# Running attention's value products and norm inside the input projection's last slab, and projecting attention first

## The chip, the cores and the metric

The kernel runs on one core of one Trainium2 chip (trn2). The metric is the device time of one execution, in microseconds. Three executions of the kernel before took 1712.12, 1700.7 and 1705.86 us, so the time before is 1705.86 us, the median. The profile and the trace come from one more execution, which took 1705.73 us.

## The reference

Two transformer blocks follow each other on a sequence of 256 tokens with 1024 features. Only the first block is touched. Cut to what matters:

```python
def first_block(x, c, ...):
    mod = jax.nn.silu(c) @ w_ada + b_ada          # six rows of 1024: shift, scale, gate, twice
    h = rms_norm(x, norm1_w) * (1.0 + scale1) + shift1
    q, k, v, cb, cc, cx, iq, ik, iw = jnp.split(h @ w_in, offs, axis=-1)
    q = rms_norm(q, q_norm_w); k = rms_norm(k, k_norm_w)
    y_attn = dsa_attention(q, k, v, iq, ik, iw)   # softmax over the chosen keys, then p @ v
    y_conv = short_conv(cb, cc, cx, conv_w, conv_b)   # cb * conv3(cc * cx)
    y_mix = jnp.concatenate([rms_norm(y_attn, attn_out_norm_w),
                             rms_norm(y_conv, conv_out_norm_w)], axis=-1)
    x = x + gate1 * (y_mix @ w_out)
    h2 = rms_norm(x, norm2_w) * (1.0 + scale2) + shift2
    return x + gate2 * peer_ffn(h2, ...)          # 8 heads x 16 experts a token out of 16384
```

`peer_ffn` multiplies `h2` by `peer_wq` (queries), takes scores against `subkeys`, chooses 16 experts a head and fetches the two rows of 1024 words of each chosen expert. The second block has modulation rows of its own (`w_ada_2`, 18 slabs), which depend only on its inputs `c` and so can be computed at any time before they are used.

## The kernel before

**Work and memory.** Activations lie feature-major, 128 features on the partitions and 256 tokens (two tiles of 128) along the free axis. Weights come in slabs of 128 x 4096 float32 words (2 MB), each a DMA on the SP queue, into a ring of four slots. SP issues the loads in one fixed order. Before most of them it waits until TensorE has read what the slot held; a load that waits holds up all loads behind it. Besides the ring, eight modulation slabs (numbers 12 and 14 to 20) are loaded into four spare homes in `arena` (`spare_slab`, home numbers in `SPARE_HOME`), by `load_spare(m)` in the same SP queue: 12 early, 14 after row 12 has been read (same home 3), 15 after the last piece of `w_in` has been read, 16 and 17 after `y_conv` and the last value product `pv3`, 19 after row 14 (home 3), 18 after row 15 (home 1), 20 after row 16 (home 2). In the code:

```python
if slabs[n][:2] == ("peer_wq", 2):
    sp.wait_ge(sem("y_conv"), 1)
    sp.wait_ge(group_done, index["pv3"] + 1)
    load_spare(16)
    load_spare(17)
    sp.wait_ge(*spare_read[14])
    load_spare(19)
    sp.wait_ge(*spare_read[15])
    load_spare(18)
    sp.wait_ge(*spare_read[16])
    load_spare(20)
```

**Rows.** `spare_row(m)` and `mod_steps` multiply one modulation slab by the condition (16 matmuls of 32 columns by 512 in the trace, since each float32 matmul shows as two passes there). `mod_turn` turns the finished rows of a group of up to four slabs back onto the partitions. Rows are filler work for TensorE: they stand wherever TensorE would wait.

**The stage of the change.** Engines run their own instruction streams, written out by hand and tied by semaphores; no scheduler moves anything. TensorE's stream ends the input projection with `cc`, `cx` and `cb` (two features-groups each; `cb` is the last slab of `w_in`). These are split products: ScalarE rounds each quarter slab (a piece) to a high part (line 1455), GpSimd subtracts it to get the low part (line 1374), and TensorE does three matmuls a block. Around them stand the attention steps: `turn_probs(t)` transposes the softmax of token tile t, `pv0` to `pv3` multiply it by the values (two heads each), `squares("conv")` and `squares("att")` sum squares for the two norms. `project` then multiplies `y_mix` by the two `w_out` slabs, tile 0 first (`wo0_0`, `wo0_1`). `second_norm(0)` sums squares of the new `x`, `query(0, 0)` makes the first queries, `turn_h(0)` transposes, `key_scores(0, 0)` makes the first scores. Then `project` does tile 1 (`wo1_0`, `wo1_1`), each releasing a `w_out` slot, into which SP loads `peer_wq` 2 and `w_ada_2` slab 9.

**The gathers.** VectorE takes the first scores and writes the first 16 expert numbers a token (`ids`, line 2413). GpSimd then issues one indirect DMA for each expert slot (line 1402): 128 rows of 8 KB, 1 MB. Eight row buffers overlay the spare homes, so the first four gathers wait until rows 17 and 18 have been copied out (`act.sem_inc`, line 1760), the next four until rows 19 and 20 have. There are 256 gathers; context slabs of the second block are loaded and multiplied in between. After the last gather the rest of the second block follows.

## Time and profile before

| | before |
|---|---|
| three executions, us | 1712.12, 1700.7, 1705.86 |
| profiled execution, us | 1705.73 |
| its span, first to last instruction, us | 1703.8 |
| TensorE busy | 1627.5 us, 96% |
| VectorE busy | 1167.1 us, 68% |
| ScalarE busy | 660.5 us, 39% |
| GpSimd busy | 389.6 us, 23% |
| chain that ended last | PE 62%, DMA 19%, DVE 10%, issue 6% |
| read from memory | 535.60 MB |

The span is 1.9 us shorter than the execution's own time; that part lies outside the instructions. PE is TensorE's matmuls and PEld its weight loads, DVE is VectorE, ACT ScalarE, POOL GpSimd, SPq the queue that issues most loads. PEclk is the granted TensorE clock as a share of full speed. "L518" is line 518 of the kernel, which is the helper `mm`, so nearly all matmuls carry it and are told apart by their tiles.

### The profile page before, as it was taken

What the parts mean: (1) busy time and instruction counts of PE and PEld (TensorE: products, weight loads), DVE (VectorE), ACT (ScalarE), POOL (GpSimd) and SP (SyncE); (2) the same over time, 40 slices, a digit from 0 to 9 for tenths busy, and PEclk for the clock granted to TensorE, in tenths of its full rate; (3) what the DMA queues carried; (4) which work ended last, traced back from release to release, by engine and by line L of the source; (5) the groups of instructions that cost most, each with busy time, mean ns of one, the idle gap of its engine ahead of it and who ended that gap; (6) DMA issues with size and microseconds to landing.
All of it is one profiled execution on the core that took longest, in us unless ns stands there. A gap on an engine that the chain in (4) does not pass through costs nothing.

```text
span 1703.8 us, 29036 instructions
## 1 busy us (share of the span) xinstructions
PE 1627.5 (96%) x11656; PEld 1464.0 (86%) x11656; DVE 1167.1 (68%) x1989; ACT 660.5 (39%) x1272; POOL 389.6 (23%) x317
## 2 busy tenths in 40 slices
PE   5999999988899899999998999999999999999997
PEld 3877889988899799998988567889998977989997
DVE  3675458778997677889788688564575456665554
ACT  3534133324433543433112158444434423444443
POOL 0553034434444434445343310000000000000000
PEclk9999999999999999999999999999999999999999
DMA  9868899999999999999999999865444522644442
GB/s 369 323 264 369 357 413 408 412 419 399 413 410 392 419 393 414 415 420 420 420 411 414 421 414 404 317 239 212 165 172 187 198 99 99 228 183 183 183 170 93
DMA packets 57732, 538.50 MB, mean 316 GB/s; under 512 B 6401, under 2 KB 6529, under 8 KB 7425
## 3 DMA queue, kind: packets, MB, share of 16 engines
q1 hardware_dynamic: 20592, 267.18, 39.5%
q0 software_dynamic: 37008, 269.50, 38.6%
q8 instruction: 92, 1.51, 0.4%
q14 instruction: 40, 0.32, 0.0%
HBM read 535.60 MB, written 1.05 MB: 315 GB/s over the span
## 4 chain that ended last, share of the span: by engine, by line
PE 62%; DMA 19%; DVE 10%; issue 6%; ACT 1%; POOL 1%; POOLq 0%; DVEq 0%; SPq 0%; ACTq 0%
PE psum L518 62%; DMA arena<-in_experts,idx_stage 16%; DVE arena L2538 4%; DVE arena L2527 1%; DMA ring<-in_w_ada 1%; POOL arena L1402 1%; DMA ring<-in_w_in 1%; DMA arena<-in_w_ada 1%; DMA extra_float<-in_w_ada 1%; DVE ring_r L2016 0%; POOL idx_stage L1395 0%; DVE arena L2649 0%; DVE small L2527 0%; DVE arena_r L2082 0%; ACT h_t L1832 0%
## 5 line engine op out<-in xcount | busy, mean ns | idle before, releaser
L2527 DVE CUSTOM_DVE_ANT_0 arena<-arena 128x1024 f32<-128x1024 f32 x256 | 313.8, 1226 | 133.5 <-DMA arena<-in_experts,idx_stage 127.4
L1402 POOL DMA_INDIRECT arena<-in_experts,idx_stage x256 | 303.8, 1187 | 365.7 <-DVE arena L2538 164.9
L2016 DVE TENSOR_TENSOR ring_r<-ring,ring_r 128x1024 fp32r<-128x1024 f32 (+1 forms) x200 | 240.7, 1214 | 197.0 <-ACT ring_r L1455 196.0
L518 PE MATMUL psum<-small_r,ring_r 128*128 128x256 f32 x1600 | 285.9, 283 | 3.4 <-DVE h_t_r L2097 3.4
L1455 ACT ACTIVATE ring_r<-ring 128x1024 fp32r<-128x1024 f32 (+1 forms) x200 | 208.2, 1048 | 170.4 <-PE psum L518 150.2
L518 PE MATMUL psum<-small,arena 128*128 128x128 f32 x2112 | 251.4, 280 | 22.0 <-ACT small L1858 21.7
L518 PEld LDWEIGHTS psum<-small,arena 128*128 128x128 f32 x2112 | 246.1, 196 | 25.9 <-ACT small L1858 23.0
L518 PEld LDWEIGHTS psum<-small_r,ring_r 128*128 128x128 f32 x1600 | 245.3, 189 | 5.4 <-issue 5.2
L518 PE MATMUL psum<-h_t,ring 128*128 128x256 f32 (+1 forms) x1360 | 248.1, 341 | 1.2 <-DMA ring<-in_w_in 1.2
L518 PEld LDWEIGHTS psum<-h_t,ring 128*128 128x128 f32 x1360 | 219.3, 191 | 21.9 <-DMA ring<-in_w_in 1.4
L518 PE MATMUL psum<-h_t_r,ring_r 128*128 128x256 f32 x800 | 223.8, 280 | 0.0
L518 PE MATMUL psum<-arena_r,ring_r 128*128 128x256 f32 x1488 | 211.6, 284 | 2.8 <-DVE arena_r L2082 2.8
L1920 ACT ACTIVATE small<-small 128x2 f32<-128x2 f32 x127 | 25.8, 203 | 463.9 <-DVE small L2527 463.8
L518 PEld LDWEIGHTS psum<-arena_r,ring_r 128*128 128x128 f32 x1488 | 192.9, 191 | 3.2 <-DVE arena_r L2082 3.2
L2538 DVE SCALAR_TENSOR_TENSOR arena<-arena,small 128x1024 f32<-128x1024 f32 x123 | 158.1, 1285 | 5.7 <-ACT small L1851 1.3
L518 PEld LDWEIGHTS psum<-h_t_r,ring_r 128*128 128x128 f32 x800 | 151.1, 189 | 0.1
L518 PE MATMUL psum<-arena,ring 128*128 128x128 f32 (+1 forms) x916 | 141.8, 316 | 0.0
L518 PEld LDWEIGHTS psum<-arena,ring 128*128 128x128 f32 x916 | 130.4, 192 | 10.7 <-issue 1.7
L518 PEld LDWEIGHTS psum<-ring 128*128 128x128 f32 x1056 | 122.9, 195 | 3.4 <-DVE ring L2478 1.9
L518 PE MATMUL psum<-ring 128*128 128x128 f32 x1056 | 123.2, 279 | 1.9 <-DVE ring L2478 1.7
L518 PE MATMUL psum<-ring_r,small_r 128*128 128x512 f32 x272 | 90.1, 399 | 0.8 <-DVE ring_r L2016 0.8
L518 PE MATMUL psum<-arena_r,upper 128*128 128x256 f32 x384 | 73.9, 295 | 9.9 <-DVE ring_r L2016 5.6
(281 smaller groups left out, 1687.6 us busy)
## 6 DMA issues: line engine op xcount, KB each, us to landing
ring<-in_w_in SPq DMA_DIRECT2D x31, 2048.0 KB, 8.6
ring<-in_w_ffn SPq DMA_DIRECT2D x29, 2048.0 KB, 11.2
ring<-in_w_ada SPq DMA_DIRECT2D x18, 2048.0 KB, 9.5
ring<-in_w_ffn SPq DMA_DIRECT2D x23, 1408.0 KB, 7.4
arena<-in_w_ada SPq DMA_DIRECT2D x8, 2048.0 KB, 16.4
ring<-in_w_out SPq DMA_DIRECT2D x4, 2048.0 KB, 9.3
ring<-in_peer_wq SPq DMA_DIRECT2D x4, 2048.0 KB, 10.3
extra_float<-in_w_ffn SPq DMA_DIRECT2D x4, 2048.0 KB, 12.5
```

The lines of the kernel that those rows point to most:

```text
L518: return nc.tensor.matmul(o, a, b, start=first, stop=last)
L1402: nc.gpsimd.indirect_dma_start(rows[slot % GBUF], None, dram["experts"], bass.IndirectOffsetOnAxis(ap=idx_stage[:, slot:slot + 1], axis=0) ...
L1455: nc.scalar.activation(upper(i), whole(i, ring), ACT.Copy).then_inc(hi_made, 1)
L1920: nc.scalar.activation(acts[:, n % 8, :], dots[:, n % 8, :], ACT.Gelu_apprx_tanh).then_inc(sem("gelus"), 1)
L2016: nc.vector.tensor_tensor(whole(i, ring_r), whole(i, ring), upper(i).bitcast(F32), ALU.subtract).then_inc(lo_made, 1)
L2527: step(nc.vector.tensor_tensor_reduce(u, u, h2[:, n // PER_TILE, :], 1.0, 0.0, ALU.mult, ALU.add, dots[:, n % 8, s:s + 1]), sem("dots"))
L2538: ins = STT(y_sum, row, weight, y_sum, ALU.mult, ALU.add)
```

## The change

TensorE now transposes both tiles' probabilities at once, right after `cx`. Then comes the first half of `cb`, then all four value products, then the second half of `cb`, then attention's squares, row 12, the convolution's squares and row 13. The output projection takes attention's blocks first. Row 14 stands behind `wo0_1`, row 15 behind `second_norm(0)`, rows 16 to 18 together behind `key_scores(0, 0)` and ahead of `wo1_0`. ScalarE's stream follows this order: it takes the two exponentials (`exp_probs`) earlier, copies the values' products out ahead of the convolution's squares, and loads the square root's table by an instruction of its own (`root_table`). Attention's squares get a place of their own (`sq_att`, where `gate_c` lay), and the convolution's root one of its own (`rstd_conv`, in `h_words`). SP's and GpSimd's instructions, and the matmuls themselves, are the same in number and in their own order.

```diff
+        sq_att = arena[:, 4096:5120].rearrange("p (j t) -> p j t", j=KA)
+        rstd_conv = h_words[:, 0:L]
...
             turn_probs(0)
-            split_feature("cb", 2, h1_hi, h_lo_1, "dve")
-            spare_row(12)
             turn_probs(1)
-            mod_steps(13, 14, False)
+            split_feature("cb", 1, h1_hi, h_lo_1, "dve")
             pe.wait_ge(*emptied("pt1_3"))
             for j in range(KA):
...
                 end(last)
-                if j == 1:
-                    squares("conv", sq1, KA, "act")
-            spare_row(14)
-            squares("att", sq1[:, KA:KD, :], KA, "act")
+            split_feature("cb", 1, h1_hi, h_lo_1, "dve", start=1)
+            squares("att", sq_att, KA, "act")
+            spare_row(12)
+            squares("conv", sq1, KA, "act")
+            mod_steps(13, 14, False)
...
                     if t == 0:
-                        pe.wait_ge(sem("y_mix"), (k - KA if k >= KA else k + KA) + 1)
+                        pe.wait_ge(sem("y_mix"), k + 1)
                     for j in range(4):
                         last = mm(o[:, j * P:(j + 1) * P], w_out[i][0][:, k, j * P:(j + 1) * P], y_mix[:, t, k, :],
-                                  k == KA and j == 0, k == KA - 1 and j == 3)
+                                  k == j == 0, k == KD - 1 and j == 3)
...
             for i in range(2):
-                project(out_banks[i], 0, i, range(KA, KD))
+                project(out_banks[i], 0, i, range(KA))
             for i in range(2):
-                end(project(out_banks[i], 0, i, range(KA)))
+                end(project(out_banks[i], 0, i, range(KA, KD)))
+            spare_row(14)
+            second_norm(0)
             spare_row(15)
-            second_norm(0)
-            spare_row(16)
...
             key_scores(0, 0)
+            spare_row(16)
+            spare_row(17)
+            spare_row(18)
             for i in range(2):
-                end(project(begin(f"wo1_{i}", "dve"), 1, i, [*range(KA, KD), *range(KA)]))
+                end(project(begin(f"wo1_{i}", "dve"), 1, i, range(KD)))
                 release(n=w_out[i][1])
-                if i == 0:
-                    spare_row(17)
-                    spare_row(18)
             spare_row(19)
...
-            for i in range(2):
-                copy_out(f"cc{i}", flat(gate_c[:, 2 * i:2 * i + 2, :]))
-            mod_steps(9, 10, False)
-            for t in range(NT):
-                exp_probs(t)
-                ahead(f"cx{t}")
+            copy_out("cc0", flat(gate_c[:, 0:2, :]))
+            ahead("cc1")
+            exp_probs(0)
+            copy_out("cc1", flat(gate_c[:, 2:4, :]))
+            mod_steps(9, 10, False)
+            exp_probs(1)
+            for i in range(2):
+                ahead(f"cx{i}")
...
+            for j in range(KA):
+                copy_out(f"pv{j}", y_att[:, j, :], width=L)
+            act.wait_ge(drained["act"], taken[0])
+            act.wait_ge(*emptied("cx1"))
+            square("att", sq_att, y_att, KA)
+            root_table()
             act.wait_ge(sem("y_conv"), 1)
             square("conv", sq1, y_conv, KA)
+            norm_root("att", ATT)
+            mod_steps(12, 13, False)
+            norm_root("conv", ATT, dst=rstd_conv)
             mod_steps(13, 14, False)
-            for j in range(KA):
-                copy_out(f"pv{j}", y_att[:, j, :], width=L)
-                if j == 1:
-                    norm_root("conv", ATT)
...
-            rooted_norm("conv")
-            mix(y_conv, KA, param("conv_out_norm_w"))
-            rooted_norm("att")
-            mix(y_att, 0, param("attn_out_norm_w"))
+            rooted_norm("att", rstd[:])
+            mix(y_att, 0, param("attn_out_norm_w"), rstd[:])
+            rooted_norm("conv", rstd_conv)
+            mix(y_conv, KA, param("conv_out_norm_w"), rstd_conv)
```

The order of the matmuls on TensorE between the input projection's last slab and the output projection, before. `arena,silu 32x512` is a row from a spare home, `ring,silu` one from the ring, `early,small` a turn, `64x128` a value product, `arena,ones` a sum of squares, `arena,ring 128x128` the output projection:

```order
L518 MATMUL psum<-arena,silu 32x512 x8
L518 MATMUL psum<-early,small 128x2 x4
L871 MATMUL psum<-early,h_t 128x128 x16
L518 MATMUL psum<-ring,silu 32x512 x8
L518 MATMUL psum<-arena 64x128 x12
L518 MATMUL psum<-arena,ones 128x256 x4
L518 MATMUL psum<-arena 64x128 x12
L518 MATMUL psum<-arena,silu 32x512 x8
L518 MATMUL psum<-arena,ones 128x256 x4
L518 MATMUL psum<-arena,ring 128x128 x64
```

The same place in the changed kernel, from the end of the last slab (its last matmul is the first row) on:

```order
L520 MATMUL psum<-arena_r,ring_r 128x256
L520 MATMUL psum<-arena,ones 128x256 x4
L520 MATMUL psum<-arena,silu 32x512 x8
L520 MATMUL psum<-early,small 128x2 x4
L520 MATMUL psum<-arena,ones 128x256 x4
L520 MATMUL psum<-ring,silu 32x512 x8
L520 MATMUL psum<-arena,ring 128x128 x64
```

The transposes (16) and value products (24) have gone ahead, into the last slab, and row 14 has gone behind the projection; rows 12 and 13 have stayed. 

TensorE from the output projection of tile 0 to that of tile 1, before. `h_t,ring` is the first query, `L969` the transposes, `arena 128x128` the first scores:

```order
L518 MATMUL psum<-arena,ring 128x128 x64
L518 MATMUL psum<-arena,silu 32x512 x8
L518 MATMUL psum<-arena,ones 128x128 x8
L518 MATMUL psum<-arena,silu 32x512 x8
L518 MATMUL psum<-early,small 128x8 x4
L518 MATMUL psum<-h_t,ring 128x128 x32
L969 MATMUL psum<-early,h_t 128x128 x8
L518 MATMUL psum<-arena 128x128 x4
L518 MATMUL psum<-arena,ring 128x128 x32
L518 MATMUL psum<-arena,silu 32x512 x16
L518 MATMUL psum<-arena,ring 128x128 x32
```

And in the changed kernel:

```order
L520 MATMUL psum<-arena,ring 128x128 x64
L520 MATMUL psum<-arena,silu 32x512 x8
L520 MATMUL psum<-arena,ones 128x128 x8
L520 MATMUL psum<-arena,silu 32x512 x8
L520 MATMUL psum<-h_t,ring 128x128 x32
L970 MATMUL psum<-early,h_t 128x128 x8
L520 MATMUL psum<-arena 128x128 x4
L520 MATMUL psum<-arena,silu 32x512 x8
L520 MATMUL psum<-early,small 128x8 x4
L520 MATMUL psum<-arena,silu 32x512 x16
L520 MATMUL psum<-arena,ring 128x128 x64
```

The row that stands alone behind the first `arena,ring` is 15 before and 14 now; the one behind the squares is 16 before and 15 now. Row 16 and the turn of rows 12 to 15 have gone behind the first scores, and rows 17 and 18 stand ahead of `wo1_0` instead of between the two halves.

## Rows read from the trace of the kernel before

**Rows 1.** The profile page's first line.

```profile
span 1703.8 us, 29036 instructions
```

**Rows 2.** Busy time by window: window, PE, PEld, DVE, ACT, POOL, PEclk, DMA, GB/s.

```profile
211.00:1040.00 829.00, 793.33 (x5348) 716.17 (x5341) 665.44 (x1270) 289.98 (x753) 328.52 (x289) 0.99 1.00 412
1040.00:1704.00 664.00, 644.28 (x4846) 595.15 (x4844) 384.56 (x497) 289.88 (x385) 0.00 (x0) 0.99 0.50 190
```

**Rows 3.** Timeline of TensorE: start, duration, operation, count, idle time before.

```profile
142.50 1.09 PE L871 MATMUL psum<-early,arena 128*128 128x128 f32 x8
...
154.95 1.92 PE L518 MATMUL psum<-arena,silu 128*32 128x512 f32 x16
...
157.72 1.95 PE L871 MATMUL psum<-early,h_t 128*128 128x128 f32 x16
...
161.45 1.53 PE L518 MATMUL psum<-arena 128*64 128x128 f32 x24
162.91 1.99 PE L518 MATMUL psum<-arena,ones 128*128 128x256 f32 x8
...
167.46 1.92 PE L518 MATMUL psum<-arena,silu 128*32 128x512 f32 x16 [1.10 <-DMA arena<-in_w_ada]
...
171.15 14.46 PE L518 MATMUL psum<-arena,ring 128*128 128x128 f32 x128
185.53 1.92 PE L518 MATMUL psum<-arena,silu 128*32 128x512 f32 x16
...
189.37 1.92 PE L518 MATMUL psum<-arena,silu 128*32 128x512 f32 x16
...
192.13 7.39 PE L518 MATMUL psum<-h_t,ring 128*128 128x128 f32 x64
```

**Rows 4.** The same timeline, later.

```profile
201.22 7.31 PE L518 MATMUL psum<-arena,ring 128*128 128x128 f32 x64
...
219.38 1.92 PE L518 MATMUL psum<-arena,silu 128*32 128x512 f32 x16
```

**Rows 5.** Timeline of VectorE.

```profile
123.99 3.88 DVE L2283 TENSOR_TENSOR h_t<-h_t,small 128x2048 f32<-128x2048 f32 x1
...
140.73 2.29 DVE L2287 TENSOR_REDUCE small<-h_t 128x8 f32<-128x2048 f32 x1 [6.85 <-ACT h_t L1685]
...
156.16 1.41 DVE L2314 TENSOR_TENSOR arena<-arena,psum 128x512 f32<-128x512 f32 x2
...
167.30 2.05 DVE L2171 SCALAR_TENSOR_TENSOR arena<-arena,prm,rstd 128x256 f32<-128x256 f32 x4
```

**Rows 6.** Timeline of VectorE at the first expert list.

```profile
211.51 0.17 DVE L2413 CAST ids<-small 128x16 uint32<-128x16 f32 x1
```

**Rows 7.** Timeline of ScalarE at the second norm.

```profile
191.32 2.44 ACT L1734 ACTIVATE h_t<-h_t,mod 128x128 f32<-128x128 f32 x8 [1.48 <-DVE h_t L2345]
```

**Rows 8.** Busy time in windows of 4 us; columns as in rows 2.

```profile
152.00:156.00 4.00, 4.00 (x38) 3.23 (x40) 3.71 (x9) 0.00 (x0) 0.00 (x0) 1.00 0.55 233
...
188.00:192.00 4.00, 4.00 (x36) 2.44 (x36) 2.02 (x6) 1.41 (x5) 0.00 (x0) 1.00 1.00 426
...
200.00:204.00 4.00, 4.00 (x37) 3.93 (x36) 1.95 (x14) 1.73 (x4) 0.00 (x0) 1.00 0.83 348
204.00:208.00 4.00, 4.00 (x38) 4.00 (x37) 3.69 (x15) 0.00 (x0) 0.00 (x0) 1.00 0.02 8
208.00:212.00 4.00, 4.00 (x37) 1.29 (x36) 3.59 (x13) 0.00 (x0) 0.00 (x0) 1.00 0.61 176
```

**Rows 9.** Timeline of the SP queue: when loads were issued.

```profile
155.05 0.33 SPq L1350 DMA_DIRECT2D ring<-in_peer_wq  x1
...
166.47 25.21 SPq L1313 DMA_DIRECT2D arena<-in_w_ada  x5
```

**Rows 10.** DMA issues of 180 to 190 us: KB, us to landing.

```profile
arena<-in_w_ada SPq DMA_DIRECT2D x1, 2048.0 KB, 12.9
```

**Rows 11.** Timeline of GpSimd at the first gather.

```profile
213.57 1.12 POOL L1402 DMA_INDIRECT arena<-in_experts,idx_stage  x1 [0.98 <-POOL idx_stage L1395]
```

More of the change, by code:

```diff
@@ L1436, in root, with norm_root @@
                 nc.scalar.activation(ap, ap, ACT.Sqrt).then_inc(sem("root_out"), 1)
-            def norm_root(tag, n=D, tokens=slice(0, L)):
-                drain(nc.scalar.activation(rstd[:, tokens], take("ss_" + tag)[:, tokens], ACT.Sqrt, bias=eps, scale=1.0 / n))
+            def norm_root(tag, n=D, tokens=slice(0, L), dst=None):
+                drain(nc.scalar.activation((rstd if dst is None else dst)[:, tokens], take("ss_" + tag)[:, tokens], ACT.Sqrt, bias=eps, scale=1.0 / n))
             hi_count = [0]
@@ L1737, in _ @@
             square_tile(0)
-            mod_steps(15, 16, False)
+            mod_steps(14, 15, False)
             second_root(0)
             second_normed(0)
-            mod_steps(16, 17, False)
+            mod_steps(15, 16, False)
             def copy_query(t, i):
@@ L1758, in _ @@
             copy_scores(0, 0)
-            mod_steps(17, 19, False)
+            mod_steps(16, 19, False)
             act.sem_inc(sem("row_free_pe"), GBUF // 2)
@@ L2167, in tile_ff_dve, with mix @@
                               ALU.mult, ALU.add))
-            def mix(src, k0, weight):
+            def mix(src, k0, weight, root):
                 for j in range(KA):
                     step(STT(y_mix[:, :, k0 + j, :], src[:, j, :].rearrange("p (t n) -> p t n", t=NT), weight[:, j:j + 1],
-                             rstd[:].rearrange("p (t n) -> p t n", t=NT), ALU.mult, ALU.mult), sem("y_mix"))
+                             root.rearrange("p (t n) -> p t n", t=NT), ALU.mult, ALU.mult), sem("y_mix"))
             def residual(names, dst, gate, per, after, sq=sq2):
@@ L2290, in normalise, with rooted_norm @@
                      sem("probs"))
-            def rooted_norm(tag):
+            def rooted_norm(tag, root):
                 v.wait_ge(*emptied("ss_" + tag))
-                step(nc.vector.reciprocal(rstd[:], rstd[:]))
+                step(nc.vector.reciprocal(root, root))
             logits(0)
```

6 lines of the change are left out of this document (removed).

## The prediction

> **What bounds the kernel now.** I read the page's first line [rows 1], then windows, then timelines of the stage that changes. From 211 to 1040 us, while the 256 expert gathers and the context slabs run, the DMA engines are busy 1.00 of the time at 412 GB/s [rows 2]. TensorE is busy 793 of 829 us there too, so two resources run side by side, but the DMA engines never pause. Behind 1040 us they are half idle (0.50) and TensorE is busy 644 of 664 us [rows 2]: a tail bound by TensorE, whose instructions the change leaves alone. Before 211 us the reader should look for holes in the DMA traffic, because a saturated phase ends when its bytes are through: a change moves the end of the kernel by as much as it changes the holes ahead of that phase. The holes stand in the 4 us windows [rows 8]: 152 to 156 is busy 0.55, 200 to 204 0.83, 204 to 208 0.02, 208 to 212 0.61. At 426 GB/s, the rate of a full window in the same rows, the three windows from 200 to 212 moved (348 + 8 + 176) x 4 us, 2.13 MB, which is 5.0 us of work, so 7.0 us are idle; the one from 152 has 1.8 us.
>
> **What a load costs.** A slab is 2.097 MB, so 4.93 us at 426 GB/s. Loads of the SP queue land in the order of issue: slab 18 was issued when row 15 had been read, at 185.53 + 1.85 = 187.4 us [rows 3], and landed 12.9 us later [rows 10], at 200.4. From 155.05, the issue of the first `peer_wq` slab [rows 9], to then the queue carried that slab, 14, the subkeys (half a slab), 15, `peer_wq` 1, 16, 17, 19 and 18, together 8.5 loads or 41.9 us, and 155.05 + 41.9 = 197.0; what is left, 3.4 us, is start and landing. So this queue had no hole, and all of it moves by as much as its first load.
>
> The Trainium skill (DMA: Bandwidth & Descriptors, Anatomy of one DMA) gives about 2.0 us fixed and then 436 GB/s for a DMA. By that the 8.5 loads take 40.9 us and slab 18 would land 1.0 us sooner than the rows say; the measured landing decides. The same skill (SBUF — State Buffer, A bandwidth-pool intuition that's wrong) says that device memory is almost always the bottleneck, at some 358 GB/s a core, which speaks against a gain from any reordering of engines; the trace agrees with the first and not with the figure, since rows 2 show 412 over 829 us.
>
> **TensorE through the stage.** Steps are timed from one row's start to the next's. The first transposes and both halves of `cb` take 154.95 - 142.50 = 12.45 us, a row 1.85 (the last to the next row's start), a turn 0.92, the 16 transposes of tile 1 1.87, each half of the value products 1.46, a sum of squares 1.9, a projected tile 14.4 [rows 3]. Changed kernel, from 142.50 on:
> - Transposes, `cb`, value products: 12.45 + 1.87 + 2.92 = 17.24, so `cb` ends at 159.75, not 154.95. This needs the probabilities of tile 1 by 143.4. Now VectorE starts their sum at 140.73, after waiting 6.85 us for ScalarE's exponential [rows 5], which stands behind a wait for a weight slab. In the new order that exponential comes ahead of the slab, and VectorE's shifted logits are ready at 123.99 + 3.88 = 127.9 [rows 5]; the exponential can end near 130. VectorE's steps for tile 1 are a sum (2.29), a small reciprocal and a product, which I bound by the 3.88 of the subtraction of the same shape; those of tile 0 have half the elements. Together 6.4 + 3.4, so done by 137.7 to 139. No wait, with 4 us of margin.
> - `y_conv` needs the second half of `cb`: VectorE's two products take 1.41 [rows 5], so the last one ends at about 160.5. The square and the root follow while TensorE does attention's squares (to 161.6), row 12 (163.45), its turn (164.4), the convolution's squares (166.2) and row 13 (168.05). Attention's root comes at 162.1, its reciprocal takes 1.75 and its four products 2.05 [rows 5], so they are done at 166.0, before the projection asks. The convolution's follow 4.5 us later and are asked for 7.2 us later. No wait; and the wait of 1.10 for slab 14 [rows 3] is gone, since row 14 is now asked for at 182.45.
> - Projection 168.05 to 182.45 (171.15 to 185.53 before: 3.1 us ahead). Row 14 takes row 15's old place, the squares end at 186.3 instead of 189.37, row 15 at 188.15.
> - The first query before had 2.76 us of cover, from 189.37 to 192.13 (row 16 and a turn). The chain from the squares to the first normed block ends at 191.32 + 0.38 = 191.7 [rows 7], 2.33 us after the squares. Now only row 15 covers it, 1.85: a new wait of 0.5. The query starts at 188.65, the first scores end at 188.65 + 9.1 = 197.75, against 201.22: 3.45 us ahead.
> - Rows 16 to 18 and a turn: 16 to 199.6, the turn to 200.5, 17 to 202.4. Row 18 then waits (below).
>
> **The loads, which are the other side.** All SP loads behind `cb` are held longer, since SP waits for the last piece of `w_in`, for row 12 and for row 13, all later now. The first goes out at 159.9 instead of 155.05: a longer hole by **+4.85 us**. Slab 14 goes out after row 12 (163.5), `peer_wq` 1 after row 13 (168.2), 16 and 17 right behind, 19 after row 14 (184.4), 18 after row 15 (188.2); each is there before the traffic ahead of it ends (17 ends about 193), so no further hole opens. Slab 18 lands at 200.4 + 4.85 = 205.2. TensorE, which wants it at 202.4, waits **2.8 us**. Row 18 ends at 207.1, `wo1_1` at 221.5, against 219.38 [rows 4]: TensorE, 3.45 us ahead at the scores, enters the gather phase 2.1 us behind. `peer_wq` 2 goes out when `wo1_0` is read, at 214.3 instead of 208.5.
>
> Slab 20 goes out after row 16, at 199.7, and its traffic ends at 203.3 + 4.85 = 208.2, the old end of traffic [rows 8] moved.
>
> The first gathers need the first expert list and the copies of rows 17 and 18. The list comes 10.5 us after the scores (211.68 - 201.2) [rows 4, 6], at 208.2 instead of 211.7; row 18 is copied at 207.8. So the list decides, and with a copy and 0.98 us behind it the first gather, issued at 213.57 before [rows 11], goes out at about 209.5; its traffic starts near 210.6. The hole there is 208.2 to 210.6, **2.4 us instead of 7.0**. Behind it four gathers (9.9 us) and `peer_wq` 2 fill the engines to 225, `w_ada_2` slab 9 (221.6) to 230, and the next four gathers go out near 227.
>
> **Sum.** Holes: +4.85 - 4.6 = **+0.3 us**. The same bytes follow. On the profiled execution, 1705.73 us with 1.9 us outside the span, that is 1706.0; on the median of 1705.86 it is 1706.2. I forecast **1706 us**, no change. The gain on TensorE and the earlier gathers are paid for by loads that start later.
>
> **Unknown costs.** How much of TensorE's 2.1 us of delay gets through lies between 0 (TensorE pauses 36 us in the 829, so it has slack) and 2.1; I take 0, nearest to the row that shows DMA at 1.00. The conflict of VectorE and GpSimd while the convolution's chain runs beside the splits may stretch that chain, but it has from 138 to 159.8 for a chain that began behind tile 1's product (143 at the earliest, 140.73 + 2.29) and ended at 156.16 [rows 5]. It would have to take 21 us instead of at most 13, so 0. Below zero: if gathers wait for their own round trip more than for bandwidth, their start 4.1 us sooner (213.57 to 209.5) counts in full, otherwise not at all; rows 2 are nearest to not at all.
>
> **Rivals.**
> - *Slower: row 18 late, and TensorE's delay counts.* The place is `spare_row(18)`; the price is 0.3 + 2.1 = 2.4 us, 1708.3, and up to 5 where slab 18 lands 3 us later still. It decides if the DMA backlog around 238 us runs out: by my sum the second four gathers end at 240.2 and the next slab's traffic starts at 239.7, a margin of half a microsecond. For it: that margin, and that TensorE is busy 96% of the phase. Against it: TensorE's 36 us of pauses.
> - *Faster: gathers bound by their own latency.* If each gather's round trip and not bandwidth sets the pace, the phase starts 4.1 us sooner: 1705.9 - 4.1 = 1701.8. For it: 19% of the chain that ended last is DMA. Against it: DMA busy 1.00 at 412 GB/s for 829 us.
> - *The transposes of tile 1 wait.* If the exponential isn't freed by the new order, TensorE stands at 143.4 until the old 146.2, 2.8 us, and `cb` and all loads behind move with it: 1706.2 + 2.8 = 1709. For it: ScalarE still stands behind one piece before it. Against it: 4 us of margin.
>
> **How the numbers follow.** A measurement of this kernel can tell about 1% (17 us) from no change, and the three executions lie within 11.4 us. Chances: forecast (within 1.5 us of 1706) 0.55, slower rival 0.22, faster rival 0.13, waiting transposes 0.06, something else 0.04. The cases reach from 1701.8 to 1709 and 1711 with the slower one's upper price; the scatter of a median of such executions adds a few microseconds at the low end. Range 1700 to 1711. No case comes to 17 us, so: faster by over 1% 0.02, within 1% 0.95, slower by over 1% 0.03.
>
> **What would show it.** The first `peer_wq` slab issued near 160 and a window before it nearly empty; no wait for `probs`; the first scores about 197.8; TensorE idle 2 to 3 us for a DMA into `arena` ahead of row 18; the first gather issued near 209.5; `wo1_1` ending near 221.5; DMA at 1.00 from 211 to 1040 and the last gather at the same time as before. I am wrong if the last gather lands more than 3 us from where it did with the DMA share still 1.00, or if TensorE's idle time in the phase grows.

## The result, and the profile of the changed kernel

The changed kernel took 1709.26 us in the median of 13 executions (1705.87 to 1716.49), the kernel before 1704.91 us in 13 executions beside it (1700.7 to 1712.12). The ratio is 1.0026, with a 95% interval of 1.0015 to 1.0038: it is 4.4 us slower, by 2.6 to 6.5. A second comparison, told below, gave 1.0049 (1.0033 to 1.0065). Both are within the 1% called "no change", and both are on the slow side of zero. The profiled execution took 1708.66 us, with a span of 1706.9 us.

TensorE's timeline in the changed kernel, the counterpart of [rows 3] and [rows 4] (start, duration, operation, count, and in brackets the idle time before it and what ended it):

```profile
159.94 1.89 PE L520 MATMUL psum<-arena,ones 128*128 128x256 f32 x8
161.76 1.92 PE L520 MATMUL psum<-arena,silu 128*32 128x512 f32 x16
...
168.28 14.56 PE L520 MATMUL psum<-arena,ring 128*128 128x128 f32 x128
...
189.10 7.38 PE L520 MATMUL psum<-h_t,ring 128*128 128x128 f32 x64 [0.57 <-ACT h_t L1736]
...
198.28 1.92 PE L520 MATMUL psum<-arena,silu 128*32 128x512 f32 x16
...
205.90 3.24 PE L520 MATMUL psum<-arena,silu 128*32 128x512 f32 x16 [2.85 <-DMA arena<-in_w_ada]
209.06 14.56 PE L520 MATMUL psum<-arena,ring 128*128 128x128 f32 x128
223.55 1.93 PE L520 MATMUL psum<-arena,silu 128*32 128x512 f32 x16
...
230.95 7.39 PE L520 MATMUL psum<-h_t,ring 128*128 128x128 f32 x64
239.07 1.92 PE L520 MATMUL psum<-ring,silu 128*32 128x512 f32 x16 [0.73 <-ACT arena L1479]
...
241.92 3.74 PE L520 MATMUL psum<-small,arena 128*128 128x128 f32 x32
```

The same place in the kernel before:

```profile
234.10 1.92 PE L518 MATMUL psum<-ring,silu 128*32 128x512 f32 x16
...
237.24 3.84 PE L518 MATMUL psum<-small,arena 128*128 128x128 f32 x32
```

The reader should see three delays in a row. TensorE stands 2.85 us for slab 18. Then row 18 takes 3.24 us, where every other row takes 1.92. And row 21, which is the `ring,silu` row at 239.07, waits 0.73 us for a copy of ScalarE. The first expert products begin at 241.92 instead of 237.24, 4.68 us later. This is where the long phase starts for TensorE.

The load queue (SP) and GpSimd's gathers, as [rows 9] and [rows 11]; the second fence is GpSimd:

```profile
160.13 0.33 SPq L1351 DMA_DIRECT2D ring<-in_peer_wq  x1
...
216.50 0.33 SPq L1351 DMA_DIRECT2D ring<-in_peer_wq  x1
223.65 0.33 SPq L1351 DMA_DIRECT2D ring<-in_w_ada  x1
```

```profile
210.61 1.12 POOL L1403 DMA_INDIRECT arena<-in_experts,idx_stage  x1 [0.98 <-POOL idx_stage L1396]
...
229.56 0.94 POOL L1403 DMA_INDIRECT arena<-in_experts,idx_stage  x1 [14.10 <-ACTq L1903]
```

The first gather goes out 2.96 us sooner than in [rows 11]; the fifth, which needs the homes of rows 19 and 20, at 229.56 instead of 225.11, 4.45 us later. So the early start is lost again within four gathers.

Busy time by window in the changed kernel, columns as in [rows 2] and [rows 8]:

```profile
152.00:156.00 4.00, 4.00 (x57) 3.83 (x52) 1.59 (x3) 2.87 (x6) 0.00 (x0) 1.00 0.68 287
156.00:160.00 4.00, 4.00 (x36) 4.00 (x35) 0.00 (x0) 1.22 (x2) 0.00 (x0) 1.00 0.00 0
...
204.00:208.00 4.00, 2.10 (x12) 0.59 (x16) 3.62 (x13) 0.00 (x0) 0.00 (x0) 0.65 1.03 438
208.00:212.00 4.00, 4.00 (x34) 2.94 (x27) 3.73 (x24) 2.10 (x3) 1.30 (x2) 0.93 0.10 41
212.00:216.00 4.00, 4.00 (x39) 4.00 (x38) 0.54 (x2) 0.00 (x0) 2.82 (x3) 1.00 0.88 297
211.00:1040.00 829.00, 790.23 (x5359) 713.78 (x5358) 657.32 (x1247) 283.84 (x746) 327.36 (x288) 0.99 1.00 410
```

To count the holes I take the bytes of four windows in a row at 426 GB/s, as in the prediction, and call the rest of the 16 us idle. From 152 to 168 it is 2.4 us before and 7.0 now, from 200 to 216 it is 7.4 before and 4.8 now; together 9.8 before and 11.8 now, 2.0 us more. In the phase the DMA share is 1.00, as in [rows 2], but 410 GB/s instead of 412. Over 829 us that is about 1.7 MB less, 4 us of traffic. The share hides this; the rate shows it. The last gather went out at 994.18 instead of 988.33.

### The profile page after: what moved, and what is told of

Its sections match the earlier page's. It is cut to its first block, busy times and chain, and to the rows that moved or that the text cites. A ratio compares the mean times of both kernels' runs of the same rounds, so it can differ in the third digit from the quotient of the medians.

```text
span 1706.9 us, 29037 instructions
## 1 busy us (share of the span) xinstructions
PE 1625.9 (95%) x11656; PEld 1459.4 (86%) x11656; DVE 1170.2 (69%) x1989; ACT 661.4 (39%) x1273; POOL 387.4 (23%) x317
## 4 chain that ended last, share of the span: by engine, by line
PE 59%; DMA 20%; DVE 11%; issue 7%; ACT 2%; POOL 1%; POOLq 0%; DVEq 0%; SPq 0%; ACTq 0%
PE psum L520 59%; DMA arena<-in_experts,idx_stage 17%; DVE arena L2540 4%; DVE arena L2529 2%; DMA arena<-in_w_ada 1%; DMA ring<-in_w_ada 1%; POOL arena L1403 1%; DMA ring<-in_w_in 1%; DMA extra_float<-in_w_ada 1%; DVE ring_r L2018 0%; DVE small L2529 0%; DVE arena L2651 0%; DVE arena_r L2084 0%; ACT h_t L1834 0%; DVE arena L2357 0%
## 5 line engine op out<-in xcount | busy, mean ns | idle before, releaser
L1456 ACT ACTIVATE ring_r<-ring 128x1024 fp32r<-128x1024 f32 (+1 forms) x200 | 208.2, 1048 | 168.4 <-PE psum L520 148.4
```

The lines of the kernel that those rows point to most:

```text
L1456: nc.scalar.activation(upper(i), whole(i, ring), ACT.Copy).then_inc(hi_made, 1)
```

## The experiments

All ratios are to the kernel before, run beside each; "us" is the ratio's distance from 1 times 1705. A ratio is estimated over all executions and isn't the quotient of the two medians, from which it differs by up to 0.0009. The first four answer whether TensorE's delay or the holes in the load traffic cost the time.

**Rows 17 and 18 back between the halves of `wo1`, all else changed.**

```diff
             spare_row(16)
-            spare_row(17)
-            spare_row(18)
             for i in range(2):
                 end(project(begin(f"wo1_{i}", "dve"), 1, i, range(KD)))
                 release(n=w_out[i][1])
+                if i == 0:
+                    spare_row(17)
+                    spare_row(18)
```

> The changed kernel with one part undone: rows 17 and 18 stand between the two halves of the tile 1 projection again, as before; everything else is as changed. Theory 1 (TensorE enters the gather phase late, 241.9 instead of 237.2 us, because row 18 waits 2.85 us for its slab and then runs at a lower granted clock): the wait goes, TensorE is level with the kernel before at the end of the projection (about 219.5), and the time is that of the kernel before, ratio 1.000 within 0.001. Theory 2 (the DMA engines carry 5 us less before 211 us, since all loads behind the last input slab start 4.85 us later): this stays as it is, the first gathers even go out at 213.5 again, so the ratio to before stays at 1.002 to 1.003.

Measured: 1704.23 us, ratio 0.9996 (0.9984 to 1.0008). TensorE's timeline of this kernel:

```profile
201.00 7.39 PE L520 MATMUL psum<-arena,ring 128*128 128x128 f32 x64
208.32 3.64 PE L520 MATMUL psum<-arena,silu 128*32 128x512 f32 x32
...
219.23 1.92 PE L520 MATMUL psum<-arena,silu 128*32 128x512 f32 x16
```

The two rows have no wait and their 3.64 us are at full clock. SP issued `peer_wq` 0 at 160.08, as late as in the changed kernel, and the first gather went out at 213.43. So the late loads stay, the first gather is back at its old time, TensorE's delay is gone, and with it the loss. But the extra holes are gone as well. Counted as above, the idle time is 7.1 + 2.4 = 9.5 us, like the 9.8 of the kernel before: the later loads now run on until `peer_wq` 2 follows them, issued at 208.42, so the second hole shrinks by as much as the first has grown. The expectation took the holes to stay as in the changed kernel, and they don't, so this run shows that the place of rows 17 and 18 is the cause, and doesn't tell TensorE's delay from the holes.

**Slab 15 loaded ahead of `peer_wq` 0, all else changed.**

```diff
+                if slabs[n][:2] == ("peer_wq", 0):
+                    sp.wait_ge(group_done, index["pt0_1"] + 1)
+                    load_spare(15)
                 if slabs[n][:2] == ("peer_wq", 1):
...
-                    sp.wait_ge(group_done, index["pt0_1"] + 1)
-                    load_spare(15)
```

> The changed kernel with the load of slab 15 issued ahead of the first peer_wq load, as soon as the transposes of tile 0 are done (about 144 us), so that it runs in the hole of DMA traffic from 154 to 162 us. Every later load lands 4.9 us sooner, slab 18 at about 201. Theory 1 (late TensorE): the wait ahead of row 18 is gone, the projection of tile 1 ends near 219.2, TensorE is 0.5 us ahead of before: ratio to before 0.999 to 1.000. Theory 2 (bytes carried ahead of the gathers): the hole is filled while the first gathers stay 3 to 4 us ahead, so 2.5 us are gained on before: ratio 0.998 to 0.999.

Measured: 1705.04 us, ratio 1.0005 (0.9996 to 1.0015). Timeline of its load queue, then of TensorE:

```profile
143.26 0.33 SPq L1314 DMA_DIRECT2D arena<-in_w_ada  x1
159.40 0.33 SPq L1352 DMA_DIRECT2D ring<-in_peer_wq  x1
```

```profile
200.39 3.64 PE L520 MATMUL psum<-arena,silu 128*32 128x512 f32 x32
...
218.45 1.92 PE L520 MATMUL psum<-arena,silu 128*32 128x512 f32 x16
```

A slab sooner in the queue, and slab 18 is there when TensorE asks. TensorE is 0.9 us ahead of the kernel before, 218.45 against 219.38 [rows 4]; 0.7 of that is this execution's, whose row 12 starts at 161.03 instead of 161.76. The first gather goes out at 209.15, near the 209.5 that I had forecast for the changed kernel. The loss is gone, but no gain takes its place. The second theory's gain of 2.5 us isn't there, and neither is what it rests on, since the hole isn't filled but moved: from 196 to 200 us the rate is now 205 GB/s instead of 418, and from 152 to 168 and 196 to 216 together 10.7 us are idle, against 9.9 in the kernel before.

**Rows 17 and 18 ahead of `wo1_0` in the kernel before.**

```diff
             key_scores(0, 0)
+            spare_row(17)
+            spare_row(18)
             for i in range(2):
...
-                if i == 0:
-                    spare_row(17)
-                    spare_row(18)
```

> The kernel before with one small part of the change: rows 17 and 18 stand ahead of both halves of the tile 1 projection. Slab 18 has landed at 200.4, so TensorE does not wait and ends the projection at 219.4 as before, but the w_out slot is read 3.6 us later, so the third peer_wq load goes out at 212.2 instead of 208.6 and the DMA traffic has a hole 3.6 us longer. Theory 1 (late TensorE): no change, ratio 1.000. Theory 2 (holes in the DMA traffic): 3.6 us slower, ratio 1.002.

Measured: 1707.09 us, ratio 1.0012 (1.0001 to 1.0024), 2.0 us. Busy time by window:

```profile
204.00:208.00 4.00, 4.00 (x39) 2.27 (x32) 3.83 (x20) 1.54 (x2) 0.00 (x0) 1.00 0.19 78
208.00:212.00 4.00, 4.00 (x38) 4.00 (x37) 3.62 (x13) 0.34 (x1) 0.00 (x0) 1.00 0.00 0
212.00:216.00 4.00, 4.00 (x38) 4.00 (x38) 3.76 (x23) 0.21 (x1) 1.62 (x3) 1.00 0.42 98
```

TensorE waits nowhere more than before, but `peer_wq` 2 is issued at 213.69 instead of 208.56, 3.6 us of it since `wo1_0` is read later and 1.5 us since this execution's row 12 starts at 156.45 instead of 154.95. The idle time from 200 to 216 is 10.3 us instead of 7.4, and with 2.5 us of the first stretch 12.8 instead of 9.8. The measured 2.0 us fit these 3.0 us of holes, but the interval reaches almost to zero. So holes aren't free; this one is likely paid for.

**20 matmuls more (4.5 us) in the second query of the kernel before.**

```diff
+                if (t, i) == (0, 1):
+                    for n, (j, k) in enumerate(order[:20]):
+                        mm(o[:, j * P:(j + 1) * P], w[:, k, j * P:(j + 1) * P], h_t[:, k, t * P:(t + 1) * P], n == 0, n == 19)
```

> The kernel before with 20 matmuls more ahead of the second query of tile 0 (the first 20 of that query made twice, the result is the same), some 4.5 us of TensorE work, behind all rows and loads of the changed stage. The first gathers, the loads up to then and the holes ahead of them stay as before; TensorE enters the gather phase 4.5 us later. Theory 1 (late TensorE): 4 to 4.5 us slower, ratio 1.0025. Theory 2 (holes): 0 to 1 us, ratio 1.000.

Measured: 1710.27 us, ratio 1.0029 (1.0019 to 1.0040), 4.9 us. TensorE's timeline:

```profile
226.80 11.86 PE L518 MATMUL psum<-h_t,ring 128*128 128x128 f32 x104
238.59 1.92 PE L518 MATMUL psum<-ring,silu 128*32 128x512 f32 x16
```

No load and none of the first eight gathers is later here (`peer_wq` 2 at 208.59, slab 9 at 219.51); TensorE alone is 4.5 us late, and the kernel takes 4.9 us longer. What comes behind is late too: the next `peer_wq` load goes out at 240.58 instead of 236.08, the ninth gather at 245.32 instead of 241.22. Busy time by window, in the kernel before and then in this one:

```profile
216.00:300.00 84.00, 83.87 (x745) 79.11 (x745) 61.62 (x164) 32.18 (x94) 31.96 (x32) 1.00 1.00 413
```

```profile
216.00:300.00 84.00, 83.87 (x745) 79.11 (x744) 57.56 (x155) 28.79 (x86) 30.42 (x31) 1.00 0.99 392
```

TensorE is as busy as before, and the DMA engines move 21 GB/s less for 84 us, 4.1 us of traffic. This is how a delay of TensorE alone becomes a delay of the loads, and it is the step that I had priced at nothing.

**20 of 32 matmuls left out of the second query, in the kernel before and in the changed one.** Only 3 of the 8 blocks of features are summed, so a part of the chosen experts differ. The same edit in both:

```diff
+                kd = 3 if (t, i) == (0, 1) else KD
-                order = [(j, k) for j in range(4) for k in range(KD)] if by_head else \
+                order = [(j, k) for j in range(4) for k in range(kd)] if by_head else \
...
```

> The kernel before, with 20 of the 32 matmuls of the second query of tile 0 left out (only the first 3 of 8 blocks of features are summed, so part of the chosen experts differ): TensorE enters the gather phase 4.5 us earlier, some 229.6 instead of 234.1 us. Theory 1 (the phase is paced by TensorE): 4 to 4.5 us faster, ratio 0.9975. Theory 2 (the phase is bound by the bytes of the DMA engines, which have little to spare): no gain or under 1 us, ratio 0.9995 to 1.000.

> The changed kernel with the same 20 matmuls left out (the same part of the second query is missing): TensorE reaches the gather phase at 234.6 instead of 239.1 us, level with the kernel before at 234.1, while the holes in the DMA traffic stay as in the changed kernel. Theory 1 (lateness of TensorE is the whole cost): ratio to before 1.000, within 0.001. Theory 2: ratio stays at 1.002 or more.

Measured: in the kernel before 1703.61 us, 0.9988 (0.9973 to 1.0002); in the changed kernel 1707.02 us, 1.0008 (0.9994 to 1.0023). The first interval holds both forecasts for it, 0.9975 and 0.9995 to 1.000, so the time doesn't decide; the trace says more. TensorE's timeline of the kernel before with the edit, then of the changed kernel with it:

```profile
227.51 2.92 PE L518 MATMUL psum<-h_t,ring 128*128 128x128 f32 x24
233.33 3.52 PE L518 MATMUL psum<-ring,silu 128*32 128x512 f32 x16 [2.90 <-DMA ring<-in_w_ada]
...
237.78 3.74 PE L518 MATMUL psum<-small,arena 128*128 128x128 f32 x32
```

```profile
224.03 1.93 PE L520 MATMUL psum<-arena,silu 128*32 128x512 f32 x16
...
237.22 3.21 PE L520 MATMUL psum<-ring,silu 128*32 128x512 f32 x16 [2.87 <-DMA ring<-in_w_ada]
```

Here the asymmetry has its reason. TensorE gets through 4.5 us sooner, then stands 2.90 us for slab 9, the slab of row 21, and takes 1.60 us longer for this row, slowly: the first products begin at 237.78, no sooner than before. The DMA issues of the kernel before from 219 to 221 us are slab 9 alone, issued at 219.48 (KB, us to landing):

```profile
ring<-in_w_ada SPq DMA_DIRECT2D x1, 2048.0 KB, 12.6
```

So the slab is there at 232.1, and TensorE reaches row 21 at 234.10, 2.0 us behind it. TensorE is the later of the two, so a delay of its own has no cover, and a lead of more than 2 us meets a wait. In the changed kernel SP can issue slab 9 only when `wo1_1` has been read, at 223.65 instead of 219.48: the delay travels by the loads as well. With the short query it is issued at 224.13, row 21 starts at 237.22 and the first products at 241.36, still 4.0 us late. The ratio of 1.0008 is what theory 1 asked for, but TensorE's delay wasn't taken away, so the run doesn't speak for it.

**40 matmuls more (9 us)**, the loop above with 40 in place of 20, the blocks beginning again after 32.

> The kernel before with 40 matmuls more at the same place instead of 20, 9 us of TensorE work. Theory 1 (TensorE paces the phase, no slack): 9 us slower, ratio 1.0053. If TensorE's pauses in the phase, 36 us of 829, absorbed part of a delay, the second 4.5 us would cost less than the first; under theory 2 the cost would begin only where the DMA backlog runs out.

Measured: 1715.27 us, ratio 1.0045 (1.0028 to 1.0061), 7.7 us (4.8 to 10.4). Twice the delay costs 1.6 times as much by the middle values; the intervals allow full and half.

**Slab 15 early and another PSUM bank for the second query.** The load's edit as above, and one bank skipped, so that row 21 doesn't come to a bank that is still being copied out:

```diff
             mod_turn(unturned.pop(0))
+            at_bank[0] += 1
             for _ in query(0, 1):
```

> The changed kernel with the load of slab 15 issued ahead of the first peer_wq load, as in the run with that label, and with the PSUM bank of the second query shifted by one, from bank 7 to bank 2. In the changed kernel the query lies in one of the two banks that are set aside for the sums of expert rows, and TensorE waits 0.73 us for its copy. Theory 1: the wait goes, TensorE is 0.7 to 1.2 us ahead of before, ratio to before 0.9993 to 1.000. Theory 2: no effect of the bank; ratio 0.998 to 0.999 by the filled hole alone, which the run without the bank shift did not show.

Measured: 1705.37 us, ratio 0.9990 (0.9977 to 1.0003). The wait of 0.73 us is gone:

```profile
234.78 1.92 PE L520 MATMUL psum<-ring,silu 128*32 128x512 f32 x16
```

It is the best version of the change that I ran, and it isn't told from the kernel before.

**TensorE's delay taken away or added ahead of the end of `wo1_1`, and the changed kernel once more.** The first edit, of the changed kernel, leaves out five of the eight blocks of `wo1_1`, 20 of its 32 matmuls; the second, of the kernel before, adds 20 whose sums are overwritten:

```diff
-                end(project(begin(f"wo1_{i}", "dve"), 1, i, range(KD)))
+                end(project(begin(f"wo1_{i}", "dve"), 1, i, [0, 1, KD - 1] if i else range(KD)))
```

```diff
             def project(o, t, i, blocks):
+                if (t, i) == (1, 1):
+                    for n in range(20):
+                        j, k = n % 4, n // 4
+                        mm(o[:, j * P:(j + 1) * P], w_out[i][0][:, k, j * P:(j + 1) * P], y_mix[:, t, k, :], n == 0, n == 19)
```

> The changed kernel, but the second half of the output projection of tile 1 (wo1_1) multiplies three of its eight blocks, so 20 of its 32 matmuls (4.5 us) are left out, and TensorE's delay is gone ahead of everything that waits for this product: the load of slab 9 into its slot, rows 19 and 20, and the gathers 4 to 7 that need these rows' homes. The loads ahead of it stay as late as in the changed kernel. Theory A, TensorE's delay is passed on by two ways, its own instructions and what it releases: both ways are closed, wo1_1 ends near 219.1, the fifth gather goes out near 225.1, slab 9 is issued near 219.2, the first expert products start near 238, and the ratio to the kernel before is 1.000 (0.999 to 1.001), below the 1.0008 of the kernel whose query was shortened behind these releases. Theory B, about a third of the loss is the holes of the loads: 1.001 or more.

> The kernel before with 20 matmuls more (4.5 us) ahead of wo1_1, whose sums are overwritten, so nothing of the result changes. TensorE is late ahead of the releases instead of behind them as in the run with 20 more in the second query. Theory A, the delay counts in full by either way: ratio 1.0027 (1.0015 to 1.004), the same as with the matmuls in the query, and the same as the changed kernel: wo1_1 ends near 223.9, fifth gather near 229.6, slab 9 issued near 224, first products near 241.7. Theory B, what hurts is the sum of late releases and a late TensorE, each in part by itself: the loads behind make it more than in the query, 1.004 or more.

> The changed kernel once more beside the other two, for the same chip and the same runs of the kernel before. All theories: 1.0026 within 1.0015 to 1.0038, which is what its first comparison gave. A ratio below 1.001 would mean that the first comparison overstated the loss and that the theories explain too much.

Measured, in this order: 1707.49 us, 1.0013 (1.0002 to 1.0024); 1710.50 us, 1.0034 (1.0021 to 1.0047); 1711.79 us, 1.0049 (1.0033 to 1.0065).

The middle one agrees with theory A: 4.5 us ahead of the releases cost 5.8 us (3.6 to 8.0), about as much as behind them; it has five executions, and its interval reaches theory B's 1.004 too. The first misses theory A's 1.000 by a little and lies where theory B had it. Its load queue and TensorE show that it doesn't decide between them:

```profile
218.60 0.33 SPq L1351 DMA_DIRECT2D ring<-in_peer_wq  x1
221.28 0.33 SPq L1351 DMA_DIRECT2D ring<-in_w_ada  x1
```

```profile
207.68 2.75 PE L520 MATMUL psum<-arena,silu 128*32 128x512 f32 x16 [2.99 <-DMA arena<-in_w_ada]
...
238.23 2.58 PE L520 MATMUL psum<-ring,silu 128*32 128x512 f32 x16 [2.27 <-DMA ring<-in_w_ada]
```

`peer_wq` 2 still goes out late, behind `wo1_0`, now 2.7 us ahead of slab 9, and slab 9 lands behind it: TensorE waits for it again. The edit took the delay out of TensorE's work but not out of the loads, and the first products are still 3.7 us late. The third is the changed kernel's second comparison, with six executions, and it misses the 1.0015 to 1.0038 that I expected. Its interval and the first comparison's overlap from 1.0033 to 1.0038. The loss is real in both, and its size is known to a factor of two. The profiled execution of this comparison was its fastest, 1703.96 us. TensorE's timeline there:

```profile
204.67 1.92 PE L520 MATMUL psum<-arena,silu 128*32 128x512 f32 x16 [2.60 <-DMA arena<-in_w_ada]
...
221.02 1.92 PE L520 MATMUL psum<-arena,silu 128*32 128x512 f32 x16
```

The wait for slab 18 is there (2.60 us), but row 18 takes 1.92 us, and the first products begin at 239.39.

**The wait for slab 18 filled with matmuls.**

```diff
             def spare_row(m):
+                if m == 18:
+                    bank = cycle[at_bank[0] % len(cycle)]
+                    if bank in tenant:
+                        pe.wait_ge(*tenant[bank])
+                    for n in range(12):
+                        mm(psum[:, bank, 0:P], ones[:], ones[:], n == 0, n == 11)
```

> The changed kernel, with 12 matmuls of ones by ones (128x128, some 2.7 us, results overwritten and never read) on TensorE ahead of its wait for slab 18. Nothing of the result changes, all loads and gathers keep their places, and row 18 starts when the slab lands, as in the changed kernel; only TensorE computes where it stood still. Theory A, only the time at which row 18 and what follows it run counts: row 18 starts near 205.9 again, and the ratio stays at what the changed kernel gave, 1.0026 or more (its two comparisons gave 1.0026 and 1.0049). Theory C, the lower granted clock behind the wait is a part of the loss (row 18 took 3.24 us at a granted clock of 0.50 in one profile of the changed kernel, 1.92 at 1.00 in another, and its executions had a mean granted clock of 0.985 against 0.986 to 0.987 of the kernel before): row 18 takes 1.92 us, wo1_1 ends 1.3 us sooner, near 222.2, the mean granted clock of the executions rises by 0.001, and the ratio falls to 1.001 to 1.002. If the filler itself is late and pushes row 18 back by more than half a microsecond, the run tells nothing between the two.

Measured: 1709.11 us, ratio 1.0019 (1.0004 to 1.0034), and a mean granted clock of 0.9861, against 0.9863 of the kernel before beside it and 0.9849 and 0.9847 in the two comparisons of the changed kernel. TensorE's timeline, then one window of this kernel and the same one of the changed kernel:

```profile
199.74 1.92 PE L526 MATMUL psum<-arena,silu 128*32 128x512 f32 x16
...
204.44 2.94 PE L526 MATMUL psum<-ones 128*128 128x128 f32 x24
207.31 1.92 PE L526 MATMUL psum<-arena,silu 128*32 128x512 f32 x16
209.16 14.56 PE L526 MATMUL psum<-arena,ring 128*128 128x128 f32 x128
```

```profile
206.00:208.00 2.00, 2.00 (x21) 1.48 (x23) 1.76 (x8) 0.00 (x0) 0.00 (x0) 1.00 0.96 410
```

```profile
206.00:208.00 2.00, 2.00 (x12) 0.48 (x16) 1.86 (x5) 0.00 (x0) 0.00 (x0) 0.50 1.08 459
```

From the start of row 16 to the start of `wo1_0` it takes 209.16 - 199.74 = 9.42 us instead of 209.06 - 198.28 = 10.78: 1.36 us sooner, with 2.9 us of work more. In the trace theory C is right: the lower clock behind the wait cost 1.3 us in the changed kernel's first profile. The measured time fits it (1.001 to 1.002 was asked for), but its interval holds theory A's 1.0026 too, so in the time it isn't told apart.

**All runs side by side.** Executions of one kernel differ by up to 2.6 us in where the stage stands already at row 12, so the delay of the first expert products is taken from row 12's start: products minus 237.24, less row 12's start minus 154.95 (161.76, as in the changed kernel's first profile, for versions of it). Of the changed kernel's 4.7 us 0.36 stand already ahead of the changed place, where its first transposes begin at 142.86 instead of 142.50, and the same is in the rows of its versions. The third column is the traffic that is missing at 300 us: the bytes from 140 us on, in windows of 4 us shifted by the same start of row 12, taken from those of the kernel before and divided by 426 GB/s.

| kernel | delay of first products, us | traffic missing at 300 us, us | measured, us (interval) |
|---|---|---|---|
| changed, first comparison | 4.7 | 4.2 | 4.4 (2.6 to 6.5) |
| changed, second comparison | 3.1 | 2.9 | 8.4 (5.6 to 11.1) |
| changed, wait filled | 3.3 | 2.9 | 3.2 (0.7 to 5.8) |
| changed, rows 17 and 18 between | 0.4 | 0.4 | -0.7 (-2.7 to 1.4) |
| changed, slab 15 early | 0.3 | 0.1 | 0.9 (-0.7 to 2.6) |
| changed, slab 15 early, other bank | -0.2 | 0.6 | -1.7 (-3.9 to 0.5) |
| changed, short `wo1_1` | 3.7 | 3.2 | 2.2 (0.3 to 4.1) |
| changed, short query | 4.0 | 3.4 | 1.4 (-1.0 to 3.9) |
| before, rows 17 and 18 ahead | -0.1 | 1.5 | 2.0 (0.2 to 4.1) |
| before, short query | -0.1 | 0.2 | -2.0 (-4.6 to 0.3) |
| before, +20 in the query | 4.4 | 4.1 | 4.9 (3.2 to 6.8) |
| before, +20 ahead of `wo1_1` | 4.7 | 4.6 | 5.8 (3.6 to 8.0) |
| before, +40 in the query | 9.1 | 8.7 | 7.7 (4.8 to 10.4) |

Ten of thirteen intervals hold the delay; two miss it by 0.1 and 0.3 us. Eleven hold the missing traffic, and one misses it by 0.1 us; it also covers the one kernel whose TensorE is on time and which still loses, rows 17 and 18 ahead. This column shows where holes and delay meet. With TensorE on time a hole ahead of the gathers is made up in part: 2.9 us are missing at 216 us and 1.5 at 300 with rows 17 and 18 ahead, 1.3 and 0.1 with slab 15 early. With TensorE late it grows: 2.4 and 4.2 us in the changed kernel, 0.0 and 4.1 with 20 matmuls more. The one far off by both is the second comparison, where one execution, the fastest of six, was profiled: a trace tells of its own execution, not of the median.

## Why the prediction came out as it did

The time of 1709.26 us lies in the range, and "within 1%" is right. That much was safe, since the range was drawn over the rivals and no case came near 17 us; the second comparison's median, 1711.79, is just outside the range. The forecast case, 1706 us with nothing moved, is not what happened: the slower rival is, at the place that it named.

- *Ahead of row 18 the steps held.* `cb` ended at 159.94 (forecast 159.75), the projection began at 168.28 (168.05), row 14's turn came at 182.77 (182.45), the new wait ahead of the query was 0.57 us (0.5), the scores ended at 198.28 (197.75). Nobody waited for `probs`.
- *The late loads held.* `peer_wq` 0 went out at 160.13 (159.9), and TensorE waited 2.85 us for slab 18 (2.8).
- *The first gather came at 210.61 (209.5)*, since row 18 was now later than the list of experts (`ids` at 208.47, forecast 208.2). The hole at 160 grew by 4.6 us (forecast 4.85), the one ahead of the gathers shrank by 2.6, where I had 4.6. So the holes sum to +2.0 us instead of +0.3.
- *The failed step* is "How much of TensorE's 2.1 us of delay gets through lies between 0 ... and 2.1; I take 0". The experiments show a delay getting through in full: 4.5 us added on TensorE alone cost 4.9 us (3.2 to 6.8), and 4.5 us ahead of the releases 5.8 (3.6 to 8.0). I took TensorE's 36 us of pauses in the phase for slack. They are elsewhere: in the kernel before TensorE is 88.87 of 89 us busy from 211 to 300, and the next thing that it needs, slab 9, has been there for 2.0 us when it comes, so nothing covers a delay. And the gathers and the next load wait for what TensorE's work sets free, so the delay becomes one of the traffic: with 20 matmuls more the ninth gather is 4.1 us late and 4.1 us of traffic are missing at 300 us.
- *The size was off as well*: `wo1_1` ended 4.17 us late (223.55 against 219.38), not 2.1. Of the difference 1.3 us is row 18 at a lower clock, and 0.7 us the slab's start at 205.90 instead of 205.2. Then 0.73 us is the wait for the PSUM bank, since the second query has slipped by one place into a bank that row 21 uses again; neither the lower clock nor the bank was in my sum. By the rival's own price, 0.3 + 2.1, it would have been 1708.3; the 4.7 us that the trace shows lie within the first comparison's 2.6 to 6.5. The holes' 2.0 us are not to be added to it: at 300 us the changed kernel lacks 4.2 us of traffic in all.
- *The faster rival* falls: with slab 15 early the first gather went out 4.4 us sooner than before (3.7 by row 12's start) and nothing was gained.
- *My own sign of being wrong*, the last gather more than 3 us late with the DMA share at 1.00, is what the trace shows: its issue is 5.9 us late, at 1.00. The execution of that trace took only 2.9 us more than the one of the kernel before, so the rest of it was shorter by 3.0 us, for which I have no reason. TensorE's idle time in the phase grew too, from 35.7 to 38.8 us.

What stays open: the holes' own price (rows 17 and 18 ahead in the kernel before, 0.2 to 4.1 us), which of the two ways of the delay carries how much, and whether the changed kernel loses 4.4 or 8.4 us.

## What to carry to other kernels

Where two resources are both over 95% busy, a busy share says nothing about slack at the entry of the phase: ask for the next thing that each will wait for, and how early it comes. Here slab 9 was 2.0 us ahead of TensorE, so a delay of TensorE counted in full, and a lead of 4.5 us went into a wait of 2.90 us and 1.60 us of slow matmuls behind it. Holes in the load traffic and a late consumer aren't two bills: count the bytes that are missing a little way into the phase, here at 300 us, which holds both. Filler work that depends on a late load isn't filler: before moving it ahead of a long product, look at the load's place in its queue, which mended this change with one slab's order.

## What was unexpected of the hardware

**Waits of TensorE of 2.3 to 3.1 us were mostly followed by slow matmuls.** The same 16 matmuls of a row took 3.24 us behind a wait of 2.85, 3.52 behind 2.90, 3.32 behind 3.09, 3.21 behind 2.87, 2.75 behind 2.99 and 2.58 behind 2.27; but 1.92 behind 2.60, and 1.92 behind the 1.10 of [rows 3]. The granted clock in the window from 206 to 208 us, behind the first, was 0.50, the lower of its two levels, and 1.00 where 12 idle matmuls filled the wait. So such a wait cost up to 1.6 us beyond its own length. For these rows it came so six times of seven; further on in the changed kernel's phase 32 matmuls of the expert products took 5.47 us behind a wait of 3.08 us, and 3.84, the full speed of them, behind one of 2.50.

**A DMA share of 1.00 at different rates.** From 211 to 1040 us the share was 1.00 at 410, 412 and, with slab 15 early, 414 GB/s. In windows of 4 us of the kernel before it is 1.00 at 426 GB/s from 144 to 148 and 1.02 at 369 from 156 to 160. So the share of time that packets take doesn't say at what rate they move.

**VectorE beside GpSimd.** The convolution's steps, which I had allowed up to 21 us, stretched, without harm. Timeline of VectorE in the changed kernel, then of GpSimd:

```profile
139.50 4.98 DVE L2311 SCALAR_TENSOR_TENSOR arena<-arena,prm 128x256 f32<-128x256 f32 x2
...
150.44 1.01 DVE L2311 SCALAR_TENSOR_TENSOR arena<-arena,prm 128x256 f32<-128x256 f32 x2
```

```profile
139.17 9.98 POOL L1375 TENSOR_TENSOR ring_r<-ring,upper 128x1024 fp32r<-128x1024 f32 x4 [5.64 <-ACT upper L1456]
```

Two operations took 4.98 us beside GpSimd's four subtractions and 1.01 us behind them. The Trainium skill (SBUF — State Buffer, SBUF: two separate sides) says that VectorE and GpSimd share one pair of ports, as an exclusive lock held for a whole instruction, also for a VectorE operation with two inputs in SBUF, if GpSimd's reads SBUF as these do; the trace agrees, with 4.98 against 1.01.
